# Feed-forward chunks 2 to 10 as pairs of 64-row products on two PSUM banks, in a two-layer encoder on one Trainium2 core

## The reference, cut to what matters

```python
def swiglu(h, w1, w3, w2):
    return (jax.nn.silu(h @ w1) * (h @ w3)) @ w2

for l in range(DEPTH):                                    # DEPTH = 2
    x = x + 0.5 * swiglu(rmsnorm(x, g_ff1[l]), w1_ff1[l], w3_ff1[l], w2_ff1[l])
    ...                                                   # attention mixer, w_o
    x = x + 0.5 * swiglu(rmsnorm(x, g_ff2[l]), w1_ff2[l], w3_ff2[l], w2_ff2[l])
return rmsnorm(x, g_final)
```

## Time and profile before

| | |
|---|---|
| median of 3 runs | 1280.29 us (1279.73 to 1281.65) |
| the profiled execution, its own time | 1279.97 us |
| its span, first to last instruction | 1278.1 us |
| TensorE busy (matmuls) | 1268.8 us, 6,823 matmuls |
| VectorE busy, ScalarE busy | 865.9 us, 684.4 us |
| granted clock of TensorE | 0.999 of full speed |

### The profile page before, as it was taken

One profiled execution on the slowest core, in us unless ns is written; L12 is line 12 of the kernel. 1 busy time (PEld: TensorE's weight loads), 2 busy tenths in 40 slices (PEclk: granted clock), 3 DMA queues, 4 the chain that ended last, 5 costly groups with the idle time before them and its releaser, 6 DMA issues.

```text
span 1278.1 us, 17726 instructions
## 1 busy us (share of the span) xinstructions
PE 1268.8 (99%) x6823; PEld 1081.9 (85%) x6823; DVE 865.9 (68%) x1244; ACT 684.4 (54%) x934; POOL 43.1 (3%) x57
## 2 busy tenths in 40 slices
PE   9999999999999999999999999999999999999997
PEld 6888888888888888888888888888888888888886
DVE  6666667656888776566675566765588887655665
ACT  6544455446766455554554544554477653644444
POOL 0411100000000000000000000000000000000000
PEclk9999999999999999999999999999999999999999
DMA  8787755574644545555445555465555454555550
GB/s 294 246 254 248 251 213 191 194 230 153 226 125 176 178 167 196 197 184 181 180 178 197 197 197 185 149 225 186 181 206 194 124 185 178 181 197 197 197 193 38
DMA packets 59213, 245.08 MB, mean 192 GB/s; under 512 B 21344, under 2 KB 27616, under 8 KB 32408
## 3 DMA queue, kind: packets, MB, share of 16 engines
q1 hardware_dynamic: 58144, 242.54, 54.5%
q10 hardware_dynamic: 984, 1.80, 0.5%
q0 software_dynamic: 32, 0.02, 0.0%
HBM read 239.07 MB, written 5.27 MB: 191 GB/s over the span
## 4 chain that ended last, share of the span: by engine, by line
PE 98%; DVE 0%; DMA 0%; issue 0%; ACT 0%; POOLq 0%; POOL 0%; SPq 0%; DVEq 0%; ACTq 0%
PE bank L738 30%; PE bank L705 17%; PE bank L706 16%; PE bank L707 16%; PE bank L742 16%; PE bank L1041 1%; PE bank L796 1%; PE bank L803 1%; PE bank L1055 1%; DMA params<-in_params 0%; DVE x L1492 0%; PE bank L891 0%; PE bank L1078 0%; PE bank L883 0%; DVE xT L1289 0%
## 5 line engine op out<-in xcount | busy, mean ns | idle before, releaser
L1153 DVE TENSOR_TENSOR wlo<-raw,whi 128x2048 fp32r<-128x2048 f32 x209 | 480.0, 2298 | 274.3 <-ACT whi L449 268.5
L449 ACT ACTIVATE whi<-raw 128x2048 fp32r<-128x2048 f32 x206 | 393.6, 1913 | 229.5 <-PE bank L742 143.3
L738 PE MATMUL bank<-xT,whi 128*128 128x512 f32 x1664 | 414.8, 391 | 0.0
L738 PEld LDWEIGHTS bank<-xT,whi 128*128 128x128 f32 x1664 | 301.8, 188 | 55.7 <-issue 0.9
L742 PEld LDWEIGHTS bank<-xT,wlo 128*128 128x128 f32 x1664 | 220.2, 190 | 12.8
L742 PE MATMUL bank<-xT,wlo 128*128 128x256 f32 x1664 | 224.1, 282 | 0.0
L705 PE MATMUL bank<-whi,xT 128*128 128x512 f32 x432 | 171.7, 398 | 0.0
L707 PE MATMUL bank<-whi,xT 128*128 128x512 f32 x432 | 168.6, 390 | 0.0
L706 PE MATMUL bank<-wlo,xT 128*128 128x512 f32 x432 | 168.3, 389 | 0.0
L705 PE MATMUL bank<-whi,hTh 128*128 128x512 f32 x320 | 124.6, 390 | 0.0
L706 PE MATMUL bank<-wlo,hTh 128*128 128x512 f32 x320 | 124.5, 389 | 0.0
(11 more groups left out here) (163 smaller groups left out, 1140.2 us busy)
## 6 DMA issues: line engine op xcount, KB each, us to landing
raw<-in_stream SPq DMA_DIRECT2D x209, 1024.0 KB, 4.8
bias<-t_rows SPq DMA_DIRECT2D x24, 256.0 KB, 6.5
bias<-in_rpb SPq DMA_DIRECT2D x16, 256.0 KB, 7.8
masked<-bias SPq DMA_DIRECT2D x8, 512.0 KB, 7.0
bias<-masked SPq DMA_DIRECT2D x8, 512.0 KB, 4.5
raw<-in_stream SPq DMA_DIRECT2D x10, 256.0 KB, 6.5
x<-in_x SPq DMA_DIRECT2D x4, 256.0 KB, 5.3
raw<-in_stream ACTq DMA_DIRECT2D x2, 256.0 KB, 4.2
```

Source lines behind the costliest of these rows:

```text
L449: act.activation(whi[:, s, :], raw[:, s, :], ACT.Copy).then_inc(hi_ready, 1)
L738: return pe.matmul(dst[blk][:, :], whi[:, s, w], xT[:, 4 * a + k, :, :].rearrange("p a s -> p (a s)"), start=start, stop=stop)
L1153: dve.tensor_tensor(wlo[:, s, :], raw[:, s, :], whi[:, s, :].bitcast(F32), ALU.subtract).then_inc(unit_split, 1)
```

## The change

The up and down units of chunks 2 to 10 (down(1) to down(9)) are issued in another form. Each matmul of 128 rows becomes two of 64 rows, one on partitions 0 to 63 and one on 64 to 127, issued one behind the other, each with its own weight load, and into different banks. A unit has four steps; in step s the lower half works on bank s of the unit's four and the upper half on bank s+2 (modulo 4), so that each bank gets both halves over the unit. Steps 2 and 3 write banks that the other half had in steps 0 and 1, and wait for the end of those on two new semaphores, `lower_done` and `upper_done`; the last step signals `unit_used` once per half. So `unit_used` counts two to a unit everywhere, and every wait on it is doubled. An up unit waits for `summed` of two banks at each of its first two steps. `half_done` comes in the last step. `copy_halves` waits for the end of the unit for all four banks, chunk 1 too. Chunks 0 and 1 and down(10) keep the 128-row form.

```diff
+        lower_done, upper_done = sem("lower_done"), sem("upper_done")
...
+        def n_used(l, u, i=0):
+            return 2 * (n_unit(l, u, i) + CREDIT)
+
+        def n_step(l, f, c, w):
+            return c * 9 + ((2 * l + f) * 9 * (CHUNKS - 2) + 3 * w - 18)
...
-                act.wait_ge(unit_used, n_unit(l, before_in_slot(u), i) + CREDIT)
+                act.wait_ge(unit_used, n_used(l, before_in_slot(u), i))
...
             def copy_halves(l, f, c, u, i):
                 for blk in range(BLK):
                     if blk == 0:
-                        act.wait_ge(half_done, n_unit(l, u, i))
+                        act.wait_ge(unit_used, n_used(l, u, i))
                     if blk == 2:
-                        act.wait_ge(unit_used, n_unit(l, u, i) + CREDIT)
                         act.wait_ge(h_split, n_chunk(l, f, c - 1))
                     part = slice(blk % 2 * S, (blk % 2 + 1) * S)
...
+            def unit_signal(last, t):
+                if t == 0:
+                    last.then_inc(half_done, 1)
+                else:
+                    last.then_inc(unit_used, 2)
...
-                    last.then_inc(half_done if t == 0 else unit_used, 1)
+                    unit_signal(last, t)
...
-                last.then_inc(unit_used, 1)
+                last.then_inc(unit_used, 2)
+
+            def in_halves(l, f, c, w, ready, products):
+
+                done = n_step(l, f, c, w)
+                for step in range(BLK):
+                    if step >= 2:
+                        pe.wait_ge(lower_done, done + (step - 1))
+                        pe.wait_ge(upper_done, done + (step - 1))
+                    else:
+                        ready(step)
+                    ends = [None, None]
+                    for product in products(step):
+                        for half in range(2):
+                            ends[half] = product(slice(64 * half, 64 * half + 64), (step + 2 * half) % BLK, half)
+                    if step < 3:
+                        ends[0].then_inc(lower_done, 1)
+                        ends[1].then_inc(upper_done, 1)
+                    else:
+                        for end in ends:
+                            end.then_inc(unit_used, 1)
+
+            def up_in_halves(l, f, c, u, i, a):
+
+                s = slot_of(u)
+                pe.wait_ge(unit_split, n_unit(l, u, i) + CREDIT)
+                dst = [bank[4 + blk] for blk in range(BLK)]
+
+                def ready(step):
+                    if a == 0:
+                        for blk in (step, step + 2):
+                            pe.wait_ge(summed, n_summed(l, f, c - 1, blk))
+                    elif step == 0:
+                        pe.wait_ge(lower_done, n_step(l, f, c, 1))
+                        pe.wait_ge(upper_done, n_step(l, f, c, 1))
+                    else:
+                        pe.wait_ge(unit_used, n_used(l, u - 1, i))
+
+                def products(step):
+
+                    def with_high(k):
+                        def go(rows, blk, half):
+                            w = slice(k * 512 + blk * P, k * 512 + (blk + 1) * P)
+                            return pe.matmul(dst[blk][:, :], whi[rows, s, w], xT[rows, 4 * a + k, :, :].rearrange("p a s -> p (a s)"),
+                                             start=a == k == 0 and step < 2, stop=False)
+                        return go
+
+                    def with_low(k):
+                        def go(rows, blk, half):
+                            w = slice(k * 512 + blk * P, k * 512 + (blk + 1) * P)
+                            last = pe.matmul(dst[blk][:, 0:S], wlo[rows, s, w], xT[rows, 4 * a + k, 0, :], start=False, stop=a == 1 and k == 3 and step >= 2)
+                            if step == 3 and k == half == 0:
+                                last.then_inc(half_done, 1)
+                            return last
+                        return go
+
+                    return [with_high(k) for k in range(4)] + [with_low(k) for k in range(4)]
+
+                in_halves(l, f, c, a, ready, products)
+
+            def down_in_halves(l, f, c, u, i):
+
+                s = slot_of(u)
+                pe.wait_ge(unit_split, n_unit(l, u, i) + CREDIT)
+                pe.wait_ge(h_split, n_chunk(l, f, c - 1))
+
+                def products(step):
+
+                    def one(j, h_part, w_part, first):
+                        def go(rows, b, half):
+                            t, n = b % 2, b // 2
+                            last = pe.matmul(bank[b][:, :], h_part[rows, j, t * P:(t + 1) * P], w_part[rows, s, j * D + n * 512:j * D + (n + 1) * 512],
+                                             start=False, stop=False)
+                            if step == 3 and first and half == 0:
+                                last.then_inc(half_done, 1)
+                            return last
+                        return go
+
+                    return [one(j, *parts, first=(j, n) == (0, 0)) for j in range(2) for n, parts in enumerate([(hTh, whi), (hTh, wlo), (hTl, whi)])]
+
+                in_halves(l, f, c, 2, lambda step: None, products)
...
                 def chunk(c, u, i):
-                    up_columns(c, u, i, 0)
-                    up_columns(c, u + 1, i, 1)
-                    down(c - 1, u + 2, i, False, False)
+                    up_in_halves(l, f, c, u, i, 0)
+                    up_in_halves(l, f, c, u + 1, i, 1)
+                    down_in_halves(l, f, c, u + 2, i)
...
-            pe.sem_inc(unit_used, CREDIT)
+            pe.sem_inc(unit_used, 2 * CREDIT)
```

More of the change, by code:

```diff
@@ L455, in to_hi_by_halves @@
                 if inside:
-                    act.wait_ge(unit_used, n_unit(l, before_in_slot(u)) + CREDIT)
+                    act.wait_ge(unit_used, n_used(l, before_in_slot(u)))
                     act.wait_ge(raw_landed[s], n_landed(l, u))
@@ L495, in h_to_hi @@
                 if down_done is not None:
-                    act.wait_ge(unit_used, down_done + CREDIT)
+                    act.wait_ge(unit_used, down_done)
                 act.activation((hTh_last if down_done is None else hTh)[:, :, :], h[:, :, :], ACT.Copy).then_inc(h_hi, 1)
@@ L503, in first_silu @@
                     else:
-                        act.wait_ge(unit_used, n_unit(l, u) + CREDIT)
+                        act.wait_ge(unit_used, n_used(l, u))
                     act.activation(silu[:, t, :], bank[t][:, 0:FC], ACT.Silu, scale=rstd[:, 0, t:t + 1]).then_inc(silu_done, 1)
@@ L553, in chunk @@
                     else:
-                        h_to_hi(l, f, c - 1, down_done=n_unit(l, u - 1, i))
+                        h_to_hi(l, f, c - 1, down_done=n_used(l, u - 1, i))
                     to_hi(l, u + 3, i)
@@ L613, in branch @@
                                 else:
-                                    act.wait_ge(unit_used, n_unit(l, u + 1, b * 2) + CREDIT)
+                                    act.wait_ge(unit_used, n_used(l, u + 1, b * 2))
                                 act.activation(v[:, b, t, :], v_bank(b, t)[:, :], ACT.Copy, scale=rstd[:, 0, t:t + 1]).then_inc(v_out, 1)
@@ L675, in _ @@
                         if b2 == BB:
-                            act.wait_ge(unit_used, n_unit(l, U_MIX + 9) + CREDIT)
+                            act.wait_ge(unit_used, n_used(l, U_MIX + 9))
                         dst, src = o_parts(b2, half)[0], o_turns(b2, half)
@@ L849, in first_two_units @@
                 for t in range(TILES):
-                    weights_lo(0, 3, t).then_inc(half_done if t == 0 else unit_used, 1)
+                    unit_signal(weights_lo(0, 3, t), t)
                 for k in range(4):
@@ L925, in down @@
                                 last.then_inc(y_done, 1)
-                        last.then_inc(half_done if n == 0 else unit_used, 1)
+                        unit_signal(last, n)
                         if last_chunk and n == 0:
@@ L1280, in ffn @@
                 split_quarter(l, following, 1)
-                dve.wait_ge(unit_used, n_unit(l, u) + CREDIT)
+                dve.wait_ge(unit_used, n_used(l, u))
                 residual(3, after_ffn=True)
```

## The result

Five runs of the changed kernel have a median of 1287.60 us (1287.06 to 1288.00), five of the kernel before on the same chip 1280.49 us: a ratio of 1.0054, 95% interval 1.0043 to 1.0065. That is 7.1 us slower, where 6.0 us faster was forecast, and outside the range of 1251 to 1283. The profiled execution took 1287.06 us, its span is 1285.3 us.

What follows compares the result with a forecast made beforehand. TensorE's own row of matmuls was taken as the bound. From 1279.97 us, -7.9 (pairs) + 1.6 (change of form) + 0.3 (copies) = -6.0 gave 1274.0 us, 0.5% faster, range 1251 to 1283.

Steps and rivals of the forecast that it cites:

- The pairs: Loop matmuls of chunks 2 to 10: 3168 pairs of halves each have 10.8 ns of gap for 13.3, 7.9 us won.
- Rival 1: Loop's wide pairs keep the full gap, 226.6 ns: 1279.0 us, or 1281.9 if narrow ones win nothing either; chance 0.22.
- The change of form: One entry to and one exit from the 64-row form per feed-forward, 8 x 0.20 us: 1.6 us lost.
- Issue and waits between steps: TensorE in the loop: doubled instructions at 0.03 us each and waits on earlier steps are covered, costing nothing.
- The copies: All four copies wait for the unit's end, 0.66 us later; covered except at the last chunk's exit: 0.3 us lost.
- Rivals 2, 3, 4 and 5: Loop: wide gap vanishes, 1252.2 us, 0.13; wide-pair stagger, 1299, 0.12; queue runs dry, 1360, 0.05; pairs run serially, about 1870, 0.02.
- Rival 3: Loop's wide pairs each pay a 10 ns stagger between halves, deciding from 1.8 ns over 226.6: 1299 us; chance 0.12.

Runs made afterwards that it cites:

- run 1: Kernel before, 128-row form kept, up units of chunks 2 to 10 in the changed kernel's order, four wide then four narrow per bank: 1284.45 us, ratio 1.0030.
- run 6: Kernel before with only the down units in 64-row halves, up units and copies as before, 72 changes of form: 1298.22 us, ratio 1.0135.
- run 5: Changed kernel with chunk 10's up units and down(9) in 128-row form, copies of chunks 1 and 10 at half the unit again: 1286.37 us, ratio 1.0042.
- run 3: Kernel before with the copies of banks 4 and 5 waiting for the unit's end alone: 1283.22 us, ratio 1.0021.
- Run 8: Full rows in run 1's order, but low products stream 384 columns in place of 256, so the output holds wrong products: 1347.74 us (one run).
- run 4: Kernel before, all narrow matmuls ahead of all wide ones in every second up unit and projection units of that form: 1278.67 us, ratio 0.9988.

## Why the prediction was wrong

**Where the 7.1 us are.** The order of wide and narrow: 3.96 us, by run 1, which repeats the loop's chunk time exactly. The eight changes of form: 8 x 0.24 = 1.9 us, by run 6's price. The late copies: what run 5 gave back, 7.1 - 5.4 = 1.7, less 4 x 0.1 = 0.4 for the four chunks whose order it also restores, 1.3 us. Sum 7.2 us. The late copies cost less here than in run 3 (2.1 by its trace), since the first of their two waits lies in the time that leaving the form takes anyway. The last two terms are differences of totals with intervals of about a microsecond each way and from two chips.

The traces fix them better. From the first matmul of down(0) to the last of down(10), summed over the four feed-forwards, the changed kernel takes 6.86 us more than the kernel before, run 1 3.85, run 5 5.18 and run 6 17.08; nearly all the rest of each difference lies ahead of the first down(0), where no matmul has changed yet. Run 1 gives 3.85 / 36 = 0.107 us a chunk for the order. Run 5 has 32 such chunks, which leaves 5.18 - 3.42 = 1.76 us for the eight changes of form (0.22 each; run 6: 17.08 / 72 = 0.24). The late copies are 6.86 - 5.18 - 0.43 = 1.25 us. By this working the three add up to 6.86; the check is that a change of form costs nearly the same here as in run 6.

**The pairs (won 7.9 us): wrong, won nothing.** The step that failed is "I take 10.8 ns, since the 128-row matmuls show the same gap at both widths". The 117.5 ns of a narrow pair are no mark of its form: full-row narrow matmuls have them too in run 1, behind slow wide ones (113.13 to 113.61 and 114.54 to 115.01, 0.47 and 0.48 for four). In settled rows wide matmuls of both forms step by 226.7 ns. Rival 1 named this: a property of the place. Its 1281.9, with nothing won by either kind, is where the sum should have stood; what the kernel took beyond that is above all the order of the widths and the reach of the late copies, below. (A slip without effect: 3.62 us over sixteen is 226.3 ns and not 226.5; the sum goes by 226.6, which a longer row gives.)

**What no term of the sum held: the order of wide and narrow.** The text costed what a matmul takes and whether the narrow ones can be issued, and never what the new order of the two does; the diff shows it (four high, four low, in every step). This is the largest term, 3.9 us, and the row that shows it stands behind the last of the earlier trace rows. The prediction held a sign of it as well: its own sum gives 16.53 us for a chunk, its last paragraph 16.58, as measured. The 0.05 us between them are the three changes from narrow to wide that the old order has.

**The change of form (1.6 us): right in place and kind, a little small.** 0.24 for 0.20: rows 5 give the two steps at the change, and not the slow matmuls behind it, which run 6 brings in. The Trainium skill, "TensorEngine Tiling (Array Packing)", section Key Properties, has such a change drain the engine. The trace has a longer step there, 0.31 to 0.34 us for 0.227, which fits; that the array is empty in between is not shown.

**Issue and waits between steps (nothing): right.** Run 1 has neither and the same chunk.

**The copies (0.3 us forecast, 1.25 us by the traces): the delay of 0.66 us was right, its reach was not.** hTl_last against the exit was worked out as it came: the step into down(10) is 0.41 us, where leaving alone has 0.31 (run 6), so 0.1 us is left of the wait. What was left out is who stands behind hTl_last on VectorE: the split of the next unit and then the residual sums that down(10)'s own transposes wait for, 0.3 us in each of three feed-forwards. I had looked for TensorE's next uses of what the chain makes, and not for what is queued behind it on VectorE.

**Rivals 2, 3, 4 and 5** did not happen. Rival 3 had the right sign, and a wide pair did come out over its threshold of 1.8 ns on average ((16.69 - 32 x 0.119) / 56 = 230 ns), but not by the stagger: run 1 has none and the same steps.
The Trainium skill, "TensorE: Matmul & The Clock Gate", section Part 3, has each further tile cost about 4 ns of the span. In a row of pairs no run here shows such a cost: run 1 and the changed kernel have the same chunk time.

**What stays open:** why wide matmuls are slow behind narrower ones, for several in a row, and why a narrow one behind a slow wide one wins a part back. Run 8 excludes one reason, none is shown. Nor is it narrow matmuls with `wlo` as weights alone: wide ones are as slow behind a change of form (run 6), and behind the transposes of down(10), already in the kernel before:

```profile
191.92 0.39 PE L706 MATMUL bank<-wlo,hTh_last 128*128 128x512 f32 x1
...
193.08 0.39 PE L705 MATMUL bank<-whi,hTh_last 128*128 128x512 f32 x1
```

These are five steps in 1.16 us, 232 ns each. So it may be the price of any break in a settled row, of which a change of width is one; no run here separates the two.

## What to carry to other kernels

Where all 128 rows are at work, as here, halving the rows won nothing: each half of the array paid the full gap at a change of weights, at the same time. Group matmuls of one width together (it won 1.8 us here), and read the step from start to start at each place where the width changes, not in one settled run of each. When a change makes a signal come later, follow the queue of each engine behind the waiting instruction to its end, next stage included.

## What the runs showed of the hardware that I had not expected

- The first four wide (512-column) matmuls behind narrower ones step by 232.5 ns on average (110.04 to 110.97), and after some more the step is 226.7 again: 0.02 us in a block of four (0.93 us for 0.91), 0.03 us for a change from narrow to wide into a long row of wide ones (run 4), in 128-row and 64-row form alike.
- A change between the 128-row and the 64-row form costs 0.24 us, counting the slower matmuls behind it (run 6).
- Two 64-row weight loads and two 64-row matmuls of 512 columns into two banks run at once at no cost in the step (0.227 us), with one behind the other in the program.
